# Projections with the activations stationary and norms with tokens on partitions, in a two-block transformer kernel

## What is computed

```
def first_block(x, ...):                       # two layers
    h = rms_norm(x, ln_mix_pre[layer])
    m = even_mixer(h, ...)                     # layer 1: odd_mixer (NSA attention and retention)
    x = x + rms_norm(m, ln_mix_post[layer])
    h = rms_norm(x, ln_ffn_pre[layer])
    x = x + rms_norm(swiglu(h, w_gate, w_up, w_down), ln_ffn_post[layer])

def second_block(x, c, ctx, c_ctx, ...):       # two layers, modulated by m = adaln(c), mc = adaln(c_ctx)
    h = half_ffn(h, m, 0, ...);  hc = half_ffn(hc, mc, 0, ...)
    y, yc = mixer(modulated_norm(h, g[2], m, 3), modulated_norm(hc, g[2], mc, 3))
    h = gated_residual(h, y, g[3], m, 3, 1.0)
    h = half_ffn(h, m, 6, ...)                 # and hc in layer 0

def rmsnorm(x, g): return x * rsqrt(mean(x * x, axis=-1) + 1e-6) * g
def swiglu_2(h, w_in, w_out): gate, up = split(h @ w_in); return (silu(gate) * up) @ w_out
def half_ffn(h, m, k, ...): return gated_residual(h, swiglu_2(modulated_norm(h, g_pre, m, k), ...), g_post, m, k, 0.5)
```

## Time and profile before

| | |
|---|---|
| median of three runs | 2719.95 us (2719.37 to 2722.16) |
| profiled execution, span | 2725.8 us |
| TensorE busy | 2528.6 us, 93% |
| VectorE busy | 1707.1 us, 63% |
| ScalarE busy | 1248.6 us, 46% |
| moved by DMA | 480 MB |

### The profile page before, as it was taken

One profiled execution on the slowest core, in us unless ns is written; L12 is line 12 of the kernel. 1 busy time (PEld: TensorE's weight loads), 2 busy tenths in 40 slices (PEclk: granted clock), 3 DMA queues, 4 the chain that ended last, 5 costly groups with the idle time before them and its releaser, 6 DMA issues.

```text
span 2725.8 us, 48854 instructions
## 1 busy us (share of the span) xinstructions
PE 2528.6 (93%) x20780; PEld 2395.9 (88%) x20780; DVE 1707.1 (63%) x2804; ACT 1248.6 (46%) x1697; POOL 1.2 (0%) x6
## 2 busy tenths in 40 slices
PE   6799997999999999999888998999999999887998
PEld 5689996888998999999887898999999999756997
DVE  6565574656766565566767576577655557646655
ACT  4443453444544444445445554455444345435443
POOL 0000000000000000000000000000000000000000
PEclk9899999999999999999898999999999999888999
DMA  6456656533555665544351344555545555363453
GB/s 218 181 200 242 241 203 229 189 109 124 186 202 216 236 226 196 211 147 154 132 174 52 120 171 154 185 175 173 179 170 179 180 177 183 114 215 137 170 178 116
DMA packets 71591, 480.14 MB, mean 176 GB/s; under 512 B 8784, under 2 KB 9296, under 8 KB 17744
## 3 DMA queue, kind: packets, MB, share of 16 engines
q1 hardware_dynamic: 66240, 468.74, 48.8%
q10 hardware_dynamic: 5136, 8.28, 1.0%
HBM read 471.48 MB, written 1.05 MB: 173 GB/s over the span
## 4 chain that ended last, share of the span: by engine, by line
PE 73%; DVE 13%; ACT 7%; DMA 4%; issue 3%; ACTq 0%; DVEq 0%
PE bank L264 64%; ACT whi L223 4%; DVE wlo L243 2%; DMA raw<-w_main 2%; DVE wlo L230 2%; PE bank L1115 2%; DMA raw<-w_down 1%; PE bank L997 1%; PE bank L935 1%; DVE ARX L686 1%; DVE HX L637 1%; DVE tmpx L631 1%; PE bank L985 1%; PE bank L553 0%; PE bank L1639 0%
## 5 line engine op out<-in xcount | busy, mean ns | idle before, releaser
L264 PE MATMUL bank<-HNX_hi,whi 128*128 128x256 f32 x2968 | 866.2, 293 | 64.3 <-DVE wlo L243 24.4
L223 ACT ACTIVATE whi<-raw 128x2048 fp32r<-128x2048 f32 (+1 forms) x378 | 705.5, 1868 | 334.6 <-PE bank L264 149.4
L264 PE MATMUL bank<-HNX_hi,wlo 128*128 128x256 f32 x2968 | 849.8, 287 | 0.0
L264 PE MATMUL bank<-HNX_lo,whi 128*128 128x256 f32 x2968 | 834.6, 286 | 0.0
L230 DVE TENSOR_TENSOR wlo<-raw,whi 128x1024 fp32r<-128x1024 f32 (+1 forms) x378 | 453.4, 1199 | 570.1 <-ACT whi L223 569.5
L264 PEld LDWEIGHTS bank<-HNX_hi,whi 128*128 128x128 f32 x2968 | 582.4, 196 | 91.7 <-issue 50.7
L264 PEld LDWEIGHTS bank<-HNX_hi,wlo 128*128 128x128 f32 x2968 | 583.1, 196 | 0.0
L264 PEld LDWEIGHTS bank<-HNX_lo,whi 128*128 128x128 f32 x2968 | 573.2, 196 | 1.1 <-issue 0.9
L243 DVE TENSOR_TENSOR wlo<-raw,whi 128x1024 fp32r<-128x1024 f32 (+1 forms) x378 | 450.8, 1193 | 0.0
L264 PE MATMUL bank<-HNC_hi,whi 128*128 128x256 f32 x1344 | 390.2, 290 | 11.6 <-DVE tmpc L448 4.5
L264 PE MATMUL bank<-HNC_lo,whi 128*128 128x256 f32 x1344 | 381.7, 284 | 0.0
(11 more groups left out here) (349 smaller groups left out, 2923.7 us busy)
## 6 DMA issues: line engine op xcount, KB each, us to landing
raw<-w_main SPq DMA_DIRECT2D x270, 1024.0 KB, 4.8
raw<-w_ada SPq DMA_DIRECT2D x72, 1024.0 KB, 4.8
raw<-w_down SPq DMA_DIRECT2D x72, 1024.0 KB, 4.9
raw<-w_down SPq DMA_DIRECT2D x36, 768.0 KB, 4.2
raw<-w_cmp SPq DMA_DIRECT2D x4, 1024.0 KB, 4.8
tmpx<-ARX ACTq DMA_DIRECT2D x18, 128.0 KB, 4.8
tmpx<-ARX ACTq DMA_DIRECT2D x32, 64.0 KB, 4.7
HX<-x_in SPq DMA_DIRECT2D x2, 512.0 KB, 6.0
```

Of the source, the lines that this page charges most:

```text
L223: NS.activation(WHI[q % HIS][:, 0:size], RAW[m % SLOTS][:, 0:size], ACT.Copy).then_inc(sems["w_hi"], 1)
L264: return NT.matmul(dst, (WHI[ordinal[n] % HIS], WLO[n % SLOTS])[w][:, k * 2 * P + col:k * 2 * P + col + P], x[xp][:, kx, :], start=start, ...
```

## The change

- `HX` and `HC` become [128, 2, 1024]: tokens on partitions, in two tiles of 128. Inputs and output have this form in memory.
- `across` (L263 in the kernel after) is a product with the activations as the stationary operand: 128 tokens stand, 512 weight columns stream for x, 256 for the context. The down projections of both lanes and all output projections use it; gate, up and the input projections keep `product` (L258).
- x's down projection reads row blocks (`w_down_x`, 11 of 1 MB per ffn in place of 12); the output projections' weights are stored as row blocks. The results add up in four banks over the whole projection. `project` runs all blocks but the last three on both tiles, then these three (`TAIL`) on tile 0 and then on tile 1, with tile 0's residual and norm in between.
- The norm sums squares along the free axis by ScalarE's `accum_out` (L494; L680 in lane C). The per-feature gain is needed as a row: `row_of` makes it by eight transposes (L484) of the broadcast gains and two copies (L487), for each of x's ffns at its third pair, for each output projection after its first block, and for the context. `scale_tile`, `turn_tile` (eight transposes L552 per tile) and `keep_tile` bring the scaled tile back to features on partitions.
- `put_out`, the totals, `spread_out` and `spread_in` are gone. x's norm yields once, 2.5 us, where it yielded 13. `first_blocks` takes the low parts two k later, not one.
- The output is stored in four pieces, two per tile.

```diff
+            def across(dst, n, at, size, k, x, xp, t, w, start, stop):
+                return NT.matmul(dst, x[xp][:, k, t * P:(t + 1) * P], (WHI[ordinal[n] % HIS], WLO[n % SLOTS])[w][:, at:at + size], start=start, stop=stop)
...
+                            if tokens:
+                                mm = across(dst, n, k * 2 * P, 2 * P, kx, x, xp, m, w, a, b)
+                            else:
+                                mm = product(dst, n, m * P, k, x, xp, kx, w, a, b)
...
-            def put_out(S, src, k, gain, *ready):
...
-                    NS.activation(S.YY if first else S.SQ[k % len(S.SQ)], src, ACT.Square).then_inc(sq.sem, 1)
-                    if k > 1:
-                        act.wait_ge(sems[f"{t}_gg_sum"], count[f"{t}_gg_sum"])
-                    NS.activation(S.GG if first else S.DIAG, src, ACT.Square, scale=gain(k)).then_inc(gg.sem, 1)
-                    NS.activation(S.Y[:, k, :], src, ACT.Copy, scale=gain(k)).then_inc(ev.sem, 1)
-                part = S.TMP[1][:, T:2 * T] if S.lag else S.TMP[0][:, 0:T]
-                if first:
...
+                        if p == 2 and not S.chunked:
+                            row_of(S, *gain, BANK[0])
...
+                        waits = {k: [lo_marks[k // 2]] for k in range(0, KF, 2)}
+                        return (yield from project(S, [("w_down_x", PAIRS * which + p) for p in pairs], S.G, waits, None, *then))
...
+            def row_of(S, gain, known, bank):
+                t, marks = S.tag, known()
+                for h in range(2):
+                    put, row = up(f"{t}_row_in"), up(f"{t}_row")
+                    if on(pe, *marks, free.get(bank.name)):
+                        for k in range(4):
+                            mm = NT.transpose(bank[:, k * P:(k + 1) * P], gain(4 * h + k).to_broadcast([P, P]), ident)
+                        mm.then_inc(put.sem, 1)
+                    if on(act, put, free.get((t, "row"))):
+                        NS.activation(S.ROW[:, h * 2 * T:(h + 1) * 2 * T], bank[:, :], ACT.Copy).then_inc(row.sem, 1)
+                    free[bank.name] = row
...
+            def residual(S, t, srcs):
+                sq, wt, re = [], [], []
+                for h, (bank, mark) in enumerate(srcs):
+                    sq.append(square_of(S, bank[:, :], SQ2[:, :], 8 * t + h, mark, now(f"{S.tag}_square")))
+                    if h:
+                        rs, root, inv = inverse(S, t, 0, sq)
+                    wt.append(up(f"{S.tag}_weighted"))
+                    if on(dve, sq[h], None if h or t else now(f"{S.tag}_row")):
+                        NV.tensor_tensor(half(S.Y, t, h), bank[:, :], S.ROW[:, h * 2 * T:(h + 1) * 2 * T], MUL).then_inc(wt[h].sem, 1)
+                    free[bank.name] = wt[h]
+                free[S.tag, "row"] = wt[1]
+                if on(dve, root):
+                    NV.reciprocal(rs, rs).then_inc(inv.sem, 1)
+                for h in range(2):
+                    re.append(up(f"{S.tag}_resid"))
+                    if on(dve, wt[h], inv):
+                        NV.scalar_tensor_tensor(half(S.H, t, h), half(S.Y, t, h), rs, half(S.H, t, h), MUL, ADD).then_inc(re[h].sem, 1)
+                return re
...
+            def scale_tile(S, t, ready):
+                sq = []
+                for h in range(2):
+                    sq.append(square_of(S, half(S.H, t, h), half(S.Y, t, h), 8 * t + 4 + h, ready[h]))
+                rs, root, inv = inverse(S, t, 4, sq)
+                if on(dve, root):
+                    NV.reciprocal(rs, rs).then_inc(inv.sem, 1)
+                sc = [up(f"{S.tag}_scaled"), up(f"{S.tag}_scaled_high")]
+                if on(dve, inv):
+                    NV.tensor_scalar(half(S.Y, t, 0), half(S.H, t, 0), rs, None, MUL).then_inc(sc[0].sem, 1)
+                if on(act, inv, ready[1]):
+                    NS.activation(half(S.Y, t, 1), half(S.H, t, 1), ACT.Copy, scale=rs).then_inc(sc[1].sem, 1)
+                return sc
...
+                    for k, src in parts:
+                        his.append(up(f"{S.tag}_hn_hi"))
+                        if on(act, turned[b]):
+                            if shift is None:
+                                NS.activation(S.HN[0][:, k, cols], src, ACT.Copy, scale=gain(k)).then_inc(his[k].sem, 1)
+                            else:
+                                NS.activation(S.HN[0][:, k, cols], src, ACT.Identity, bias=shift(k), scale=gain(k)).then_inc(his[k].sem, 1)
+                    for k, src in parts:
+                        if shift is None:
+                            los.append(up(f"{S.tag}_hn_lo"))
+                            if on(dve, his[-1]):
+                                NV.scalar_tensor_tensor(S.HN[1][:, k, cols], src, gain(k), S.HN[0][:, k, cols].bitcast(fp32), MUL, SUB).then_inc(los[k].sem, 1)
+                            free[bank.name] = los[k]
+                            continue
...
+                def part(n, b, t):
+                    for h in range(2):
+                        bank, last = acc[t][h], b == nb - 1
+                        if b == 0:
+                            on(pe, free.get(bank.name))
+                        for j in range(2):
+                            if on(pe, *waits.get(2 * b + j, ()) if t == h == 0 else ()):
+                                for w, xp in ((0, 0), (0, 1), (1, 0)):
+                                    mm = across(bank[:, :], n, j * D + h * 2 * T, 2 * T, 2 * b + j, x, xp, t, w,
+                                                b == j == 0 and (w, xp) == (0, 0), last and j == 1 and w == 1)
+                        if last and (t, h) != (1, 1):
+                            marks[t, h] = up(f"{S.tag}_tile")
+                            if pe:
+                                mm.then_inc(marks[t, h].sem, 1)
+                    if t == 1 and pe:
+                        mm.then_inc(sems["block_done"], 1)
+                for b in range(nb - TAIL):
+                    yield ("D",)
+                    n = take(S.tag, *blocks[b])
+                    landed(n)
+                    part(n, b, 0)
+                    splits(n, apart=True)
+                    opened[0] = S.tag
+                    yield ("d",)
+                    opened[0] = None
+                    part(n, b, 1)
+                    other_half()
+                    if b == 0 and row:
+                        row_of(S, *row, BANK[4])
+                known = mods()
+                yield ("D",)
+                ns = [take(S.tag, *blocks[b]) for b in range(nb - TAIL, nb)]
+                opened[0] = S.tag
+                table_of(ACT.Sqrt)
+                for j, n in enumerate(ns):
+                    landed(n)
+                    part(n, nb - TAIL + j, 0)
+                    if j == 0:
+                        splits(n)
+                    yield ("d",)
+                first = residual(S, 0, [(acc[0][h], marks[0, h]) for h in range(2)])
+                if pre:
+                    first_scaled = scale_tile(S, 0, first)
+                for j, n in enumerate(ns):
+                    if j == TAIL - 1 and pre:
+                        turned = turn_tile(S, 0, first_scaled)
+                        keep_tile(S, 0, turned, pre, known)
+                    part(n, nb - TAIL + j, 1)
+                    if j < TAIL - 1:
+                        splits(n + 1)
+                        yield ("d",)
+                opened[0] = None
+                marks[1, 1] = done(ns[-1])
+                free["x", "y"] = marks[1, 1]
+                second = residual(S, 1, [(acc[1][h], marks[1, h]) for h in range(2)])
                 if not pre:
-                    if dve:
...
+                inv = inverses(S.H, 4, ready)
+                sc = [up(f"{t}_scaled"), up(f"{t}_scaled_high")]
+                if on(dve, inv):
+                    NV.tensor_scalar(S.Y[:, 0, :], S.H[:, 0, :], N[:, 6:7], None, MUL).then_inc(sc[0].sem, 1)
+                if on(act, inv):
+                    NS.activation(S.Y[:, 1, :], S.H[:, 1, :], ACT.Copy, scale=N[:, 7:8]).then_inc(sc[1].sem, 1)
+                yield ("L", 6.0)
+                for j in range(2):
+                    x = keep_tile(S, j, turn_tile(S, j, [sc[j]] * 2), pre, mods)
+                    yield ("L", 5.0)
+                free[t, "dst"] = [x[1][-1]]
...
-                x = yield from norm(X, True, (gain1("ffn_pre", 0), None), y[-1:], then=ACT.Tanh)
-                yield from ffn(X, 0, gain1("ffn_post", 0), x)
-                y = [now("x_evac")]
-                x = yield from norm(X, True, (gain1("mix_pre", 1), None), y)
+                x = yield from out_of("ev_out", {k: [mixed[k]] for k in range(KD)}, of_vec("mix_post", 0), (gain1("ffn_pre", 0), None), then=ACT.Tanh)
+                x = yield from ffn(X, 0, x, of_vec("ffn_post", 0), (gain1("mix_pre", 1), None))
```

533 lines of the change are left out of this document (195 added, 338 removed).

## The result

The changed kernel takes 2788.45 us (median of 4 runs, 2786.87 to 2792.32) where the kernel before takes 2720.14: a ratio of 1.0251, 95% interval 1.0236 to 1.0265, 68 us slower. The forecast was 2733, with a range up to 2775. The side was right and the size was a fifth of the real one. The profiled execution spans 2787.6 us against 2725.8, so the two traces differ by 61.8 us.

A forecast was written before the change was run, and what follows sets the result against it. It took TensorE (busy 93%) to bound the kernel. Terms −42 + 22 + 26 − 6 − 5 − 8.4 + 15 + 20 − 3 − 5 = +13 on the median 2719.95 gave 2733 us, range 2662 to 2775.

The forecast's parts named there:

- The side: Whole kernel: the change makes it slower, chance 0.51, against 0.40 for faster and 0.09 for within measurement error.
- part 2: Work added on TensorE: 264 short transposes at 0.112 us, less context totals and spreads removed; +22 us.
- the rows of gains: `row_of`'s second four transposes wait for ScalarE's copy of the first, in x's ffns, projections and context places; +20 us.
- the end: After the last product: table loaded before, short norm on half a tile, 14.6 us become 6.2; −8.4 us.
- the context norm ahead of the GQA keys: Its chain of about 21 us stands exposed, with nothing between its transposes and the products needing it; +15 us.
- the term of −6: Kernel opening: first product 3 us earlier, and another 3 from faster hi and lo parts; −6 us.
- part 1: x's down and output projections: 3936 products of 256 columns become 1968 of 512 at 0.216 us; −42 us.
- part 3: Norm of tile 1 at nine places: 130 us lost, against 104 before, with splits ahead in the queues; +26 us.
- small gains, −8: Output projections wait for one k at a time, −3 us; `put_out` gone, so VectorE is late less often, −5 us.
- Exposure doubles: Rival: rows of gains and context norm at upper ends, tail at its bad end; 2779 us, chance 0.10.
- The first: Rival: tile 1's chain meets free engines, nine norms lose 52 us; 2655 us, gain below 13.0 per norm, chance 0.37.

The follow-up runs named there:

- 5.0: Changed kernel with x's norm yielding 5.0 in place of 2.5, so 96 context products, not 48, stand before tile 1's transposes at most places: ratio 1.0147, −28 us.
- 7.0: Changed kernel with x's norm yielding 7.0 in place of 2.5 (144 context products) and the row of gains made in two banks: ratio 1.0155.

## Why the prediction was right or wrong

**Right:** the side; the order of the queues at the tail and the 12 us from the last product to the transposes; the transposes added (352 of them, about 0.108 us each, where part 2 had 0.112); the rows of gains (32.5 forecast, 34 measured for 12 of the 14 rows); the end, where 14.6 became 6.0 us from the last product's start to the span's end (6.2 forecast); that the context norm ahead of the GQA keys is exposed whole (+15 forecast, about +17 to +20 by its waits). The opening came 2 us earlier at the first product and not 3, but 5.9 earlier at the 96th (30.89 against 36.81), which agrees with the term of −6.

**Wrong, the price of a wide product** (part 1, "I take 216, close to the lower end, since the 13 ns that go beyond the columns today are covered once there are 213 ns of columns to cover them"). They are not covered: 227 ns is again the columns and 13 to 14. So work fell by 26 us and not 47, and the run by 16 and not 42. By the Trainium skill, page "TensorE: Matmul & The Clock Gate", section "Back-to-back issue gap", an isolated product of 512 columns takes about 216 ns and a sustained one 131; this trace shows 227 in a dense stretch, above both. What the 13 ns are stays open.

**Wrong, and as large: the context work moved out of x's norms** (part 3, where a norm's price is what is lost inside its stretch and nothing else). As a sum over the nine stretches part 3 came out on the good side: 257.73 us with 1166 products lose 118 us after by the reckoning that gave 104 before, a term of +14 where **+26** was forecast. But the stretches after hold 48 context products or none where before up to 240 stood in one, and the sum took the products that moved away as free to stand anywhere. They are not. The kernel before with the same few yields is 51 us slower, with more than half of the added waits outside the stretches, and half of the way back (5.0) gives the changed kernel 28 us, of whose waits again more fell outside (186 to 168) than inside (82 to 78). Put beside that run (1.0187), the changed kernel is 17 us slower and not 68. That is a reckoning and not a measurement of the share: the 51 are those of the old norm, and how much of them the new one has is not known, since with 7.0 the changed kernel loses again. By what path each of the waits outside comes from the moved work stays open.

**Wrong, "small gains, −8", and what stands around them.** Nothing of it can be seen. Waits for lo halves of weights rose by 14 us. The two longest after, 6.0 us at 198.10 and 5.4 at 921.14, are places where VectorE has eight scalings and four subtractions of a context norm (L587, L567; 4.3 us) between the two lo halves of a block. And 7 us are waited for the bank of the odd mixer's rotations, 5.3 of it at 427.66, where two lo halves and two products (L1447) stand ahead of the rotation on VectorE.

**A price from the wrong engine.** Part 3 took a hi part of 128 columns at 0.28 us from a row of VectorE (L1585), though ScalarE makes it. The eight at 1008.66 take 2.87 us, 0.36 each. That is 0.6 us for eight and changes no conclusion.

**Of the rivals,** the one nearest the result was "Exposure doubles" (2779, chance 0.10). The first, with the chance of 0.37, needed the tail to be hidden; its point of decision, 13.0 us lost per norm, was reached (118 / 9 = 13.1), by which the kernel should have come out near 2720, and it was 68 us slower. So the sum around that term was wrong, and not the term. That the side was right is in part luck: with the tail at its measured 118 the sum would have been 2721, no change at all, and it was the steps the sum had too low that made the kernel slower. The range failed because all its bounds were bounds of single terms, and none was set for work that is moved out of a stretch.

## What to carry to other kernels

Where one chain's gaps are filled by another's work, that work has a value by its place: an edit that shortens the chain and takes its filling out at the same time should be priced by putting only the second half into the old kernel first, and by looking for the loss outside the chain as well as in it. Give the new chain about as much filling as it has length: 48 products were too few here, 144 ran into the filling's own chain, 96 was best of the three. Swapping two queue entries that the next stage needs both only renamed a wait here.

## What the runs showed of the hardware that was not expected

A product of 256 columns takes 120 ns start to start and one of 512 takes 227, at full clock with one 128 x 128 load each: 13 to 14 ns beyond the columns in both. At half clock nothing is left beyond them: the wide product goes at 0.43 us (2011.15, 2011.58 and 2012.01 in the run with one tail block, granted clock 0.50), which is 512 columns at 1.2 GHz, and the other at 0.21. A square with its sum (L494) is 0.60 us for 512 columns and is followed by a read of the accumulator of 0.19 to 0.24 us that is an instruction of its own in ScalarE's timeline. Hi parts of 128 columns start 0.34 us apart where they take a scale and a bias from memory (L577, eight in 2.87 us) and 0.25 where they take a scale alone (L575). The two also differ in the function, Identity and Copy, and no run parts the two causes; the forecast took 0.28 for all.
